# Two stored expert rows per token, or one row of sums that the DMA adds up: a mixture-of-experts step on one core

## What is computed

```python
h2 = (rms_norm(x, norm2_g) * (1 + scale2) + shift2).reshape(n * l, d)
idx, wts = hier_route(h2, w_rg, b_rg, w_re, b_re)      # two experts and two weights per token
y = routed_experts(h2, idx, wts, w_gate, w_up, w_down) # sum of the two weighted expert outputs
x = x + gate2 * y
# one expert: (silu(x @ w_gate[e]) * (x @ w_up[e])) @ w_down[e];  a final rms_norm follows
```

## Time and profile before

| | us |
|---|---|
| median of 3 runs (2307.08 to 2308.64) | 2308.5 |
| the profiled execution | 2307.37 |
| its span, from first to last instruction | 2305.9 |
| `experts`, from its first POOL instruction on the blocks to its last copy (1577 to 2173) | 596 |
| `combine` (2178.3 to the end) | 127.6 |

### The profile page before, as it was taken

The page is one execution under the profiler, slowest core; times in us unless marked ns, Lnnn a source line. Parts: engine busy times, 40 slices in busy tenths (PEclk is TensorE's granted clock), DMA queues, the critical chain, the costliest instruction groups (busy, mean ns, idle before and its releaser), DMA issues. The chain is left out here.

```text
span 2305.9 us, 28759 instructions
## 1 busy us (share of the span) xinstructions
PE 1992.8 (86%) x9169; PEld 1423.8 (62%) x9170; DVE 879.8 (38%) x1859; ACT 514.6 (22%) x1114; POOL 264.2 (11%) x406
## 2 busy tenths in 40 slices
PE   5699999999689999992999999954999999999600
PEld 2588888888567777762888888732444444444300
DVE  3466666666230000014355555542111111111188
ACT  2244444444030000003111111100111111111111
POOL 0000000000000000000001110011111111111165
PEclk9799999999699999996999999976999999999855
DMA  8322122222185454527344334307998454879486
GB/s 277 119 94 77 75 91 84 93 93 83 45 302 201 163 204 163 204 62 248 136 146 156 135 136 146 100 26 236 336 388 297 152 203 148 308 260 368 180 304 236
DMA packets 185655, 407.95 MB, mean 177 GB/s; under 512 B 27774, under 2 KB 107134, under 8 KB 180610
## 3 DMA queue, kind: packets, MB, share of 16 engines
q1 hardware_dynamic: 157540, 312.26, 39.0%
q0 software_dynamic: 20880, 69.03, 8.2%
q10 hardware_dynamic: 7200, 26.22, 2.8%
HBM read 296.47 MB, written 110.99 MB: 177 GB/s over the span
## 5 line engine op out<-in xcount | busy, mean ns | idle before, releaser
L1982 PE MATMUL ex<-expert_ring,gathered_T 128*128 x816 | 361.1, 596 | 4.2 <-SPq L1818 2.9
L1982 PEld LDWEIGHTS ex<-expert_ring,gathered_T 128*128 128x128 f32 x816 | 151.8, 191 | 177.3 <-issue 177.3
L265 PE MATMUL mix<-w_mix_hi,hT_hi 128*128 128x512 f32 (+3 forms) x544 | 204.4, 376 | 3.9 <-DVE hT_lo L645 2.6
L267 PE MATMUL mix<-w_mix_lo,hT_hi 128*128 128x512 f32 (+3 forms) x544 | 198.8, 365 | 0.0
L266 PE MATMUL mix<-w_mix_hi,hT_lo 128*128 128x512 f32 (+3 forms) x544 | 198.4, 365 | 0.0
L2003 PE MATMUL ex<-expert_ring,hidden_T 128*128 x400 | 179.9, 592 | 0.0
L1933 DVE SCALAR_TENSOR_TENSOR silu_e<-tanh_e,ex 128x256 f32<-128x256 f32 x51 | 21.5, 421 | 352.5 <-ACT tanh_e L1888 352.5
L1155 DVE SCALAR_TENSOR_TENSOR ma_rows<-tanh_rows,ga 128x512 f32<-128x512 f32 (+1 forms) x34 | 21.8, 683 | 337.0 <-PE ga L267 186.6
L265 PE MATMUL gb<-w_b_hi,h_parts_b 128*128 128x512 f32 (+1 forms) x272 | 109.2, 401 | 27.8 <-DVE w_b_lo L1450 18.6
L265 PE MATMUL ga<-w_a_hi,h_parts 128*128 128x512 f32 (+1 forms) x272 | 109.2, 401 | 17.3 <-DVE w_a_lo L1140 14.7
L2003 PEld LDWEIGHTS ex<-expert_ring,hidden_T 128*128 128x128 f32 x400 | 72.1, 190 | 71.7 <-issue 71.7
(11 more groups left out here) (302 smaller groups left out, 3279.0 us busy)
## 6 DMA issues: line engine op xcount, KB each, us to landing
expert_ring<-in_w_gate SPq DMA_DIRECT2D x32, 1024.0 KB, 8.8
expert_ring<-in_w_up SPq DMA_DIRECT2D x32, 1024.0 KB, 12.4
expert_ring<-in_w_down SPq DMA_DIRECT2D x32, 1024.0 KB, 14.3
expert_rows<-y_block ACTq DMA_DIRECT2D x50, 512.0 KB
h_parts<-hT_split SPq DMA_DIRECT2D x16, 1024.0 KB, 5.1
mixer_parts<-oT_split SPq DMA_DIRECT2D x32, 512.0 KB, 8.3
w_ada_part<-in_w_ada SPq DMA_DIRECT2D x16, 1024.0 KB, 10.8
h_parts_b<-hT_split SPq DMA_DIRECT2D x16, 1024.0 KB, 4.9
```

The costliest lines, as they stand in the source:

```text
L265: nc_mm(out, left[0], right[0], start=first, stop=False)
L267: return nc_mm(out, left[0], right[1], start=False, stop=last)
L1982: last = nc.tensor.matmul(ps[2 + par][:, :], xT[par][:, k, :], w[:, bass.ds(slot * WC + k * 2 * EH, 2 * EH)], start=(k == 0), stop=(k == K ...
```

## The change

Each token gets one row in a new DRAM tensor `expert_sums` ("y"), with 128 spare rows behind them. POOL zeroes it in `sweep_gate_a`. The routing table holds three numbers per slot: the token to gather (or one past the last, for an unused slot), the row to add to (a spare row, for an unused slot), and the weight. In `experts` ACT and DVE multiply by the weight while they copy from PSUM, and POOL adds the block to `expert_sums` with an indirect DMA that accumulates. Of an unused slot nothing is gathered. In `combine` ACT loads 128 consecutive rows of sums per tile, and DVE only multiplies by the gate and adds x. What found the two rows per token (the kept experts, ranks and weights, the last steps of `list_blocks`, the zeros over unused blocks) is gone.

```diff
@@ sweep_gate_a, gpsimd
+            def clear(i, m=P):
+                pool.dma_start(s["y"][bass.ds(i * P, m), :].rearrange("p (n d) -> p n d", n=2),
+                               zero[0:m, :].unsqueeze(1).to_broadcast([m, 2, 512])).then_inc(filled, 16)
                     store(p * 2 + par, par, P)
+                    clear(p * 2 + par)
             store(NT, 0, MS)
+            clear(NT)
+            clear(NT + 1, MS)
+            pool.wait_ge(filled, 16 * (NT + 2))
@@ sweep_gate_b, gpsimd
-            pool.memset(zero, 0).then_inc(setup, 1)
-            for n in ("wts", "eid", "rank"):
-                pool.memset(kept[n][:, :, :], 0.0).then_inc(setup, 1)
-            pool.dma_start(s["table"].rearrange("(p c) o -> p (c o)", p=P), zero).then_inc(filled, 16)
+            pool.dma_start(s["table"], a["empty"]).then_inc(filled, 16)
-                                            in_=ids[0:m, :], in_offset=None).then_inc(scattered, 16)
+                                            in_=rec[0:m, k, :], in_offset=None).then_inc(scattered, 16)
@@ sweep_gate_b, vector: route, rank
-                step(nc.vector.tensor_copy(kept["eid"][0:m, bass.ds(i, 1), :].rearrange("p o k -> p (o k)"), r[0:m, 114:116]))
-                step(nc.vector.tensor_copy(kept["wts"][0:m, bass.ds(i, 1), :].rearrange("p o k -> p (o k)"), r[0:m, 118:120]))
-                step(nc.vector.tensor_copy(kept["rank"][0:m, bass.ds(i, 1), :].rearrange("p o k -> p (o k)"), r[0:m, 120:122]))
-                step(nc.vector.tensor_copy(ids[0:m, :], idf[0:m, :]))
+                step(nc.vector.tensor_copy(rec[0:m, :, 0], idf[0:m, :].to_broadcast([m, 2])))
+                step(nc.vector.tensor_copy(rec[0:m, :, 1], idf[0:m, :].to_broadcast([m, 2])))
+                step(nc.vector.tensor_copy(rec[0:m, :, 2].bitcast(F32), r[0:m, 118:120]))
@@ experts, gpsimd
-            pool.memset(zero[:, :], 0.0).then_inc(zeroed, 1)
+            pool.wait_ge(cleared, 1)
             def gather(b, par, n, first=False):
-                                        in_offset=bass.IndirectOffsetOnAxis(ap=idx[:, par:par + 1].bitcast(U32), axis=0)).then_inc(x_in[par], 16)
+                                        in_offset=bass.IndirectOffsetOnAxis(ap=idx[:, par, 0:1].bitcast(U32), axis=0),
+                                        bounds_check=TOKENS - 1, oob_is_err=False).then_inc(x_in[par], 16)
+            def records(b, slot, before):
+                if before is not None:
+                    wait_apart(pool, stored[slot % 2], before, passed)
+                row = listed(pool, 2, b)
+                pool.dma_start(rec[:, slot, :], s["table"][bass.ds(row, P), 1:3]).then_inc(rec_in[slot], 16)
+            def scatter(b, slot, before):
+                if before is not None:
+                    wait_apart(pool, stored[1 - slot % 2], before, passed)
+                wait_apart(pool, y_a, b + 1, passed)
+                wait_apart(pool, y_d, b + 1, passed)
+                pool.indirect_dma_start(out=s["y"], out_offset=bass.IndirectOffsetOnAxis(ap=rec[:, slot, 0:1].bitcast(U32), axis=0),
+                                        in_=y[:, slot % 2, :], in_offset=None, compute_op=ALU.add).then_inc(stored[slot % 2], 16)
+            def step(b, slot, n, before, earlier):
+                gather(b + 2, slot % 2, n)
+                records(b + 1, (slot + 1) % 4, before)
+                scatter(b - 1, (slot - 1) % 4, earlier)
@@ experts, scalar
-                nc.scalar.copy(y[:, par, 0:512], ps[5][:, :]).then_inc(y_a, 1)
-                act.wait_ge(y_a, b + 1)
-                act.wait_ge(y_d, b + 1)
-                act.dma_start(s["ys"][bass.ds(b * P, P), :], y[:, par, :]).then_inc(stored[par], 16)
+                act.wait_ge(rec_in[slot], landed)
+                nc.scalar.activation(y[:, slot % 2, 0:512], ps[5][:, :], ACT.Copy, scale=weight(slot)).then_inc(y_a, 1)
@@ experts, vector
+            nc.vector.memset(xg[:, :, :], 0.0).then_inc(cleared, 1)
-                nc.vector.tensor_copy(y[:, par, 512:1024], ps[6][:, :]).then_inc(y_d, 1)
+                dve.wait_ge(rec_in[slot], landed)
+                nc.vector.tensor_scalar(y[:, slot % 2, 512:1024], ps[6][:, :], weight(slot), None, ALU.mult).then_inc(y_d, 1)
@@ combine, gpsimd: gather is gone, rms stays; scalar
+            def sums(i, k, m):
+                act.dma_start(g[0:m, k, :], s["y"][bass.ds(i * P, m), :]).then_inc(g_in[k], 16)
@@ combine, vector
-                nc.vector.tensor_copy(wt2[0:m, k, :], kept["wts"][0:m, bass.ds(i, 1), :].rearrange("p o k -> p (o k)")).then_inc(wt_ready, 1)
-                nc.vector.tensor_scalar(o[0:m, k, :], g[0:m, k, 0, :], wt2[0:m, k, 0:1], None, ALU.mult).then_inc(weighted, 1)
-                nc.vector.scalar_tensor_tensor(out=o[0:m, k, :], in0=g[0:m, k, 1, :], scalar=wt2[0:m, k, 1:2], in1=o[0:m, k, :],
-                                               op0=ALU.mult, op1=ALU.add).then_inc(weighted, 1)
-                nc.vector.tensor_tensor(o[0:m, k, :], o[0:m, k, :], gate[0:m, :], ALU.mult).then_inc(weighted, 1)
+                nc.vector.tensor_tensor(o[0:m, k, :], g[0:m, k, :], gate[0:m, :], ALU.mult).then_inc(weighted, 1)
```

More of the change, by code:

```diff
@@ L1750, in _ @@
             step(nc.vector.tensor_tensor_scan(ends[:, :], n[:, :], zero[:, :], 0.0, ALU.add, ALU.add))
-            step(nc.vector.tensor_tensor(starts[:, :], ends[:, :], n[:, :], ALU.subtract))
             step(nc.vector.tensor_copy(ends_i[:, :], ends[:, :]))
@@ L1830, in _ @@
             sp.wait_ge(lists_in, 32)
-            def unused(p, total):
-                with sp.If(p * 2 < total):
-                    sp.sem_inc(filled, 16)
-                with sp.If(p * 2 >= total):
-                    rows = s["ys"][bass.ds(p * (2 * P), 2 * P), :].rearrange("(q two) d -> q (two d)", two=2)
-                    sp.dma_start(rows, zero[:, :]).then_inc(filled, 16)
-            sp.wait_ge(zeroed, 1)
-            assert PAIRS == NE and RING * 2 <= NE
-            total = listed(sp, 3, 0)
             with sp.Fori(1, NE // RING) as g:
@@ L1878, in _ @@
+            for par in range(2):
+                wait_apart(pool, stored[par], (total + 1) // 2 * 16, passed)
         @block.scalar
@@ L1906, in _, with step @@
             total = listed(act, 3, 0)
-            def step(b, par, before):
+            def step(b, slot, landed, before):
+                par = slot % 2
                 hidden(b - 1, 1 - par)
@@ L1911, in step @@
                 turned(b + 1, 1 - par)
-                store(b - 1, 1 - par, before)
-            step(1, 1, None)
-            step(2, 0, None)
-            with act.Fori(1, PAIRS) as p:
-                with act.If(p * 2 < total):
-                    step(p * 2 + 1, 1, p * 16)
-                    step(p * 2 + 2, 0, p * 16)
-            for par in range(2):
-                wait_apart(act, stored[par], (total + 1) // 2 * 16, passed)
+                weigh(b - 1, (slot - 1) % 4, landed, before)
+            step(1, 1, 16, None)
+            step(2, 2, 16, None)
+            step(3, 3, 16, 16)
+            step(4, 0, 16, 16)
+            with act.Fori(1, QUADS) as q:
+                with act.If(q * 4 < total):
+                    step(q * 4 + 1, 1, q * 16 + 16, q * 32)
+                    step(q * 4 + 2, 2, q * 16 + 16, q * 32)
+                with act.If(q * 4 + 2 < total):
+                    step(q * 4 + 3, 3, q * 16 + 16, q * 32 + 16)
+                    step(q * 4 + 4, 0, q * 16 + 16, q * 32 + 16)
         @block.vector
         def _(dve):
+            nc.vector.memset(xg[:, :, :], 0.0).then_inc(cleared, 1)
             dve.wait_ge(lists_in, 32)
@@ L2120, in _ @@
             for k in range(NB):
+                sums(k, k, P)
+            for k in range(NB):
                 tile(k, k, P, k == 0)
-            with act.Fori(1, GROUPS) as p:
+                sums(NB + k, k, P)
+            with act.Fori(1, GROUPS - 1) as p:
                 for k in range(NB):
                     tile(p * NB + k, k, P)
+                    sums(p * NB + NB + k, k, P)
+            for k in range(NB):
+                tile(NT - NB + k, k, P)
+                if k == 0:
+                    sums(NT, 0, MS)
             tile(NT, 0, MS)
```

141 lines of the change are left out of this document (63 added, 78 removed).

## The result

The changed kernel takes 2321.8 us (median of 5 runs, 2316.4 to 2327.9) where the kernel before takes 2308.5. The ratio of the means is 1.0066, 95% interval 1.0040 to 1.0091; one execution of the kernel before that fell in a slow state (2791 us) is left out of it. So it is slower by 0.7%; the forecast was 2280. The profiled execution after has a span of 2326.2 us where before had 2305.9. Read by stage, those 20.3 us are

The account below looks back on a forecast made before the run. PE bounds `experts`; POOL's order of work bounds `combine`. 2307.4 - 40.1 (`combine`) + 8 (PE waiting) + 2.7 + 1.4 (stage ends) = 2279.4, with 1.1 for the median 2280 us; its own range 2262 to 2300.

Parts of the forecast that it names:

- combine: Last stage: 14.0 us start, 16 tiles of 4.0 and the end, 87.5 us in place of 127.6, a gain of 40.1.
- Rival A: `combine` is bound by DMA at 4.5 us a tile, the rest as forecast: 2288 us; chance 0.10.
- D: Rival: the scatter costs PE nothing and DVE alone sets `combine` (tile 3.86 us): 2268 us; chance 0.09.
- Then the step is 8.8 + 2.9 = 11.7, 0.3 over the period: POOL's step per block in `experts` against PE's 11.40 us: 31 blocks, 8 us of PE waiting, ends 0 and 118.
- The hold: In `experts`, how long the scatter's rows keep the token list back in POOL's queue: 3.5 us, ends 1.5 and 7.
- rival B: In `experts` the list waits behind the scatter's rows and POOL's step sets the period: 2325 us at 5 us hold; chance 0.16.
- The rule on the source reads: For the scatter in `experts`: free add, halved rate, so a hold of 3.0 us, step 11.2, time about 2272 us.
- The clock: In `experts`, PE's 11.40 us per block hold only at a granted clock of 1.00; a fall makes the prediction wrong.
- Exit of `experts`: From the last copy to `combine`, 5.0 us before: later issue and landing of the scatter add 2.7, ends 0.6 and 7.
- Exit of `sweep_gate_a`: Two clears behind POOL's last store add 1.0 us of issue and a 0.5 MB write: 1.4 us, ends 0 and 3.
- The fill of the table: In `sweep_gate_b`, the larger fill has 76 us of waiting behind it, so 0; failure would show as a late first norm.
- Rival C: In `experts` each scatter waits for the landing of the one before: 2432 us at a landing of 14 us; chance 0.15.

Follow-up runs that it names:

- plain_scatter: The changed kernel with the add taken from the scatter of `experts` (rows stored, not summed); 2284.1 us, 0.990 of the kernel before.
- list_own_queue: The changed kernel with the token lists issued by ACT on its own queue, behind its half of the block's result; 2275.6 us, 0.986 of the kernel before.
- list_own_late: list_own_queue with each of ACT's lists held back until POOL counts the scatter as issued; 2276.9 us, 0.987 of the kernel before.
- stage_starts: list_own_queue with the clears of `sweep_gate_a` moved ahead of its stores and the slot table's fill moved to that stage's start; 2273.3 us.
- own_queue_plain: list_own_queue with the add taken from the scatter, so rows are stored, not summed; 2274.6 us, one run.

## Why the prediction was wrong

**combine: right.** 86.7 us against 87.5 forecast. The mechanism held, the closeness is in part luck: two terms were off and cancelled. The start took 16.6 us (14.0 forecast; it waits for the last constant, as before), 2.6 more; the tile 3.82 (4.0 forecast), 2.9 less over 16 tiles, with a gap of 0.44 us for the norm's chain at every second tile. Rival A, bound by DMA, is out; D's tile was the better one.

**experts: the step that failed.** It is the sentence "Then the step is 8.8 + 2.9 = 11.7, 0.3 over the period". The mechanism was named and its direction was right; every term of the sum was a little short. Over the 29 blocks with a long wait (31 before, as forecast) POOL's step has a mean of 13.5 us:

| term, us | forecast | measured |
|---|---|---|
| wait for the list | 8.25 | 8.8 |
| issue of the scatter | 1.0 | 1.62 |
| issue of the list behind it | 0.57 | 0.6 to 1.0 |
| issue of the gather | 0.98 | 1.07 |
| records, gaps | 0.87 | 1.1 to 1.3 |
| step | 11.7 | 13.5 |

The hold, the term that the prediction called unknown, came out near its value: the waits grew by 3.6 us with weights in flight and by 2.7 without (5.27 to 8.84, 2.52 to 5.18), which with the 0.6 between scatter and list makes holds of 4.2 and 3.3 where 3.5 was taken. (By the packets some 0.6 us of it isn't the queue's order but the traffic beside the list, which the prediction didn't separate.) What was not seen is how little room there was. The other blocks have a step of 10.9 us, only 0.5 under PE's 11.40, so they give back little: from list to list the mean is 12.4 us, and PE's transposes follow each other in 12.3. POOL's queue sets the period of the whole stage. 50 blocks at 0.9 us more are 45 us; `experts` lost 44. So rival B is what happened: it priced a step of 13.2 us and a time of 2325, and had 0.16. The point from which it was said to turn the sign, a hold of 4.4 us, was worked out with the other terms at their low ends. Without its hold the measured step is 13.5 - 4.2 = 9.3 us, so it is over PE's period from a hold of 2.1 us on. In plain_scatter, with cheaper issues and a hold of 2.7, the mean step is 11.5: just at it.

**The source for the scatter's issue.** It was taken from the indirect gathers, 0.98 us. plain_scatter shows that this was right for a scatter (1.02); the add makes it 1.62. The sum gave this term one value and no range.

**The rule on the source reads.** By the Trainium skill ("Collectives: The Full Stack", The bandwidth ceiling: the fold count and why AG ≠ RS ≠ AR) the add itself costs no time, and its second source read halves the rate. In the packets the rate is about halved: a row of 4 KB took 0.33 us with the add and 0.16 without. The list's first bytes moved 3.0 us behind the scatter's with the add and 1.6 without; told by POOL's waits, the hold went from 2.7 us to 4.2. But the add wasn't free on the issuing engine: it took 0.6 us more of POOL for each scatter. So the 2272 us that the prediction worked out by this rule alone missed by more than the forecast did.

**The clock.** The prediction said that it would be wrong at once if the granted clock fell from 1.00. It fell, but as a consequence: in list_own_queue, with the same accumulates and no waits, it is 1.00. With the 27 us of waiting came 17 us of longer matmuls, and no term of the sum held them.

**Stage ends.** Exit of `experts`: +2.7 forecast, +9.5 measured. The landing was judged well: without the drain the exit is 8.2 us, and 5.0 + 2.7 is 7.7. What was missing comes behind it: a drain of 6.35 us that ran under the last blocks before, since POOL had nothing to do with the results, and now follows the last scatter. Exit of `sweep_gate_a`: +1.4 forecast, +3.8 measured: 1.3 of issue, 1.5 of a longer drain, the rest the landing of the clears. The fill of the table, counted at 0 with its cover named as the 76 us before the first norm, delayed instead the second set of weight loads, which started 11.1 us into the stage (9.1 before); up to its last scatter the stage grew by 2.3 us. `list_blocks` and the first list grew by 1.4 us, also counted at 0; why wasn't tried.

**Rival C** didn't happen. The accumulates land 9.5 us after their issue starts (10.4 at most), and POOL never waited for one. That is not far from 11.40: a landing 1 to 2 us longer would have been a second bound.

**What remains open.** What a queue of its own is worth to a list that goes out as late as in the changed kernel (list_own_late let it out 0.7 us earlier); why a stage with its POOL DMAs at its start ended later (stage_starts and the three kernels built on it); and what sets the length of POOL's drain behind the changed `experts`. The last also makes the exit of plain_scatter longer than that of own_queue_plain (14.2 and 10.0 us): the two differ by 4.2 us, and their drains, of 8.97 and 4.31 us, by 4.7.

## What to carry to other kernels

When a DMA is moved to a queue, list what stands behind it there and ask how long each small transfer in the new order waits for a large one: the 1.5 KB list behind 0.5 MB of added rows cost 44 us, and moving the list, not the rows, gave all of it back. Compare the step of the issuing engine with the period of the bounding one term by term, and give each term its high end: where the margin is a tenth of the period, small errors of one sign decide. And ask of each engine what it does after its last instruction: work that moves an engine's end behind the last result exposes its clean-up as well.

## What the runs showed of the hardware

- An accumulating scatter of 128 rows of 4 KB takes 1.62 us of POOL to issue, a storing one 1.02, and the small DMA issued next on the same engine 0.6 to 1.0 instead of 0.56. A row of 4 KB took 0.33 us of a DMA engine with the add, 0.16 without. The accumulate landed after 9.5 us (storing 7.9), and a small transfer behind it on its queue waited 2.7 to 3.6 us longer than with none. Issued 0.7 us earlier and on another queue, that transfer landed after 5.3 us (median) instead of 8.0, but the longest was the same 9.4.
- POOL's drain at a stage's end took 2.83, 4.32, 4.40 and 8.56 us after 34, 52, 53 and 104 DMAs issued by POOL, 82 to 83 ns for each. After an earlier drain it takes 0.14 to 0.55. A drain with transfers in flight held POOL for 4.0 to 9.5 us, until just behind the landing of the last one issued. At the end of the changed `experts`, with 208 DMAs, it was 6.35 us, and 8.97 with stored rows, so there the price isn't 83 ns for each; what sets it stays open.
- Six waits of PE of 2.2 to 3.0 us were followed by eight transposes at 1.97 us instead of 1.04 (seven others, of 0.2 to 4.1 us, by 1.09 to 1.33), and in stretches with such waits the granted clock was 0.95 to 0.99.
